# Squares of queries and keys one step later, GpSimd's weight additions ahead of modulation row loads

## The reference

```python
q = apply_rope(rmsnorm(heads(q, N_HEADS_A), qn), cos, sin) * scale
k = apply_rope(rmsnorm(heads(k, N_KV_A), kn), cos, sin)
...
s = jnp.einsum('bqhgd,bkhd->bhgqk', qi, k_all)
p = softmax_f32(s, v_all.dtype)
```

## Time and profile before

| | us |
|---|---|
| median of 3 runs | 2938.09 |
| lowest and highest | 2937.65 and 2938.37 |
| the profiled execution | 2939.53 |
| its span, first to last instruction | 2937.7 |
| TensorE busy | 2817.2 |
| VectorE busy | 1363.4 |
| ScalarE busy | 770.1 |
| GpSimd busy | 225.2 |

### The profile page before, as it was taken

The page is one execution under the profiler, slowest core; times in us unless marked ns, Lnnn a source line. Parts: engine busy times, 40 slices in busy tenths (PEclk is TensorE's granted clock), DMA queues, the critical chain, the costliest instruction groups (busy, mean ns, idle before and its releaser), DMA issues.

```text
span 2937.7 us, 33851 instructions
## 1 busy us (share of the span) xinstructions
PE 2817.2 (96%) x13312; PEld 1523.4 (52%) x13312; DVE 1363.4 (46%) x2569; ACT 770.1 (26%) x1410; POOL 225.2 (8%) x253
## 2 busy tenths in 40 slices
PE   7999899999999999999999989999999999999998
PEld 3555555655555655576444644444445734444442
DVE  2696776775355674674485741111115813121112
ACT  3334454441222453433251120000003232000001
POOL 2233212100011010000000000000002300000000
PEclk9999999999999999999999999999999999999999
DMA  8244222111145443112110158999993217999996
GB/s 315 90 162 153 91 73 87 37 73 58 79 155 169 135 152 106 44 46 89 63 61 20 56 216 359 421 421 422 421 420 145 107 67 299 410 421 422 421 421 282
DMA packets 90673, 586.60 MB, mean 200 GB/s; under 512 B 10192, under 2 KB 10192, under 8 KB 29232
## 3 DMA queue, kind: packets, MB, share of 16 engines
q1 hardware_dynamic: 69696, 502.56, 42.6%
q0 software_dynamic: 20848, 82.26, 8.4%
HBM read 582.68 MB, written 2.10 MB: 199 GB/s over the span
## 4 chain that ended last, share of the span: by engine, by line
PE 68%; DVE 6%; ACT 2%; issue 1%; DVEq 0%; ACTq 0%
PE BIG L1097 43%; PE PJ L1097 11%; PE BIG L1941 4%; PE PT L1426 2%; PE PT L1442 2%; DVE ARENA L2984 1%; PE PT L1097 1%; PE BIG L1409 1%; PE PJ L1146 1%; PE BIG L1413 1%; PE PT L1917 1%; DVE ARENA L3036 0%; DVE ARENA L3035 0%; ACT ARENA L2145 0%; PE BIG L1402 0%
## 5 line engine op out<-in xcount | busy, mean ns | idle before, releaser
L1097 PE MATMUL BIG<-ARENA 128*64 128x512 f32 (+3 forms) x2720 | 565.4, 458 | 6.5 <-DVE ARENA L3058 2.5
L1097 PEld LDWEIGHTS BIG<-ARENA 128*64 128x64 f32 (+1 forms) x2720 | 302.2, 169 | 255.4 <-issue 224.3
L1097 PE MATMUL PJ<-HT,W 128*128 128x512 f32 (+2 forms) x1040 | 400.3, 533 | 7.3 <-DVE ARENA L2694 2.6
L1097 PE MATMUL BIG<-W,ARENA 128*64 128x512 f32 (+1 forms) x1280 | 282.0, 573 | 0.9 <-DVE ARENA L2906 0.9
L1097 PEld LDWEIGHTS PJ<-HT,W 128*128 128x128 f32 x1040 | 193.8, 193 | 166.3 <-issue 127.9
L3087 DVE SCALAR_TENSOR_TENSOR XC<-BIG,MOD,XC 128x512 f32<-128x512 f32 x128 | 90.2, 747 | 379.4 <-PE BIG L1941 379.4
L2156 ACT ACTIVATE ARENA<-PT 128x512 f32<-128x512 f32 (+1 forms) x264 | 145.1, 583 | 416.8 <-PE PT L1426 416.5
L1097 PE MATMUL BIG<-HT,W 128*128 128x512 f32 (+1 forms) x600 | 236.6, 553 | 2.4 <-DVE ARENA L2860 2.1
L1097 PEld LDWEIGHTS BIG<-W,ARENA 128*64 128x64 f32 (+1 forms) x1280 | 107.4, 142 | 161.0 <-issue 154.9
L2723 DVE TENSOR_REDUCE STAT<-BIG 128x1 f32<-128x512 f32 (+5 forms) x240 | 169.9, 724 | 39.2 <-PE BIG L1413 34.2
L1097 PE MATMUL BIG<-HT,ARENA 128*64 128x512 f32 (+1 forms) x632 | 182.9, 573 | 0.0
(11 more groups left out here) (325 smaller groups left out, 3068.4 us busy)
## 6 DMA issues: line engine op xcount, KB each, us to landing
ARENA<-in_exp_w SPq DMA_DIRECT2D x168, 1024.0 KB, 18.1
W<-in_exp_w SPq DMA_DIRECT2D x144, 1024.0 KB, 16.7
W<-in_units SPq DMA_DIRECT2D x89, 1024.0 KB, 4.9
HT<-in_exp_w SPq DMA_DIRECT2D x72, 1024.0 KB, 21.9
ARENA<-in_mod_rows POOLq DMA_DIRECT2D x76, 512.0 KB, 4.5
W<-in_mod_rows POOLq DMA_DIRECT2D x52, 512.0 KB, 4.5
ARENA<-in_bias_b POOLq DMA_DIRECT2D x16, 384.0 KB, 4.9
XC<-in_x SPq DMA_DIRECT2D x1, 3072.0 KB, 10.1
```

The lines of the kernel that those rows point to most:

```text
L1097: ins = pe.matmul(out, lhsT, rhs, start=start, stop=stop, skip_group_check=skip)
```

## The change

In `block_slots` an item "square" no longer takes the place of its turn: it is put into the step behind that of the item before it, at most `room - 1`, and the norm that follows it comes no earlier than that step. Items behind the square keep their places. In GpSimd's list each unit's additions are sorted 16 places before the end of position 5 of the unit before, instead of at it; what they wait for stays the same.

```diff
@@ block_slots
     room = tiles if PAIRS[i][0] == "B" else tiles - 1
+    squared = 0
...
             least = before + 1
             continue
+        if item[0] == "square":
+            squared = min(before + 1, room - 1)
+            out.append((squared, item))
+            continue
+        if item[0].startswith("norm_"):
+            at = least = max(at, squared)
         out.append((at, item))
         before = at
@@ gpsimd program
+            ADDED_AHEAD = 16
             jobs = [(row_place(x)[0], 1, x) for x in range(len(MOD_ROWS))]
...
             for u in range(len(uses)):
-                jobs.append((uses[u - 1][5][1] if u else -1, 3, u))
+                jobs.append((uses[u - 1][5][1] - ADDED_AHEAD if u else -1, 3, u))
```

## The result

The changed kernel took 2947.86 us (median of five runs, 2947.69 to 2953.07) against 2938.09 us: a ratio of 1.0039, 95% interval 1.0028 to 1.005. It is slower by about 9.8 us; 13.7 were forecast, and the range of 2944.0 to 2958.0 holds the time. The profiled execution took 2947.69 us with a span of 2945.9, so it is 8.16 us longer than that of before. In the changed kernel the numbers of the lines are 8 higher than before (L1097 is L1105, L2091 is L2099, L2156 is L2164, L2177 is L2185, L1354 is L1362, L2613 is L2621); on GpSimd they are 7 higher (L1007 is L1014).

A forecast was written before the change was run, and what follows sets the result against it. TensorE, busy 96% of the span, was taken as the bound, so its waits decide. Terms 8.3 + 2.8 - 0.8 + 2.1 + 1.3 = +13.7 us gave 2951.8 us against the median of 2938.09, range 2944.0 to 2958.0.

The forecast's parts named there:

- the main term: Layer 0, second modulation vectors: their load goes behind unit 7's additions, ScalarE's Silu starts 8.3 us late, TensorE takes it all.
- the squares win: Rival, pairs 5 to 7: second norm matmul starts about 0.8 us sooner in each; 2947.6 us in all; chance 0.06.
- vectors that are late but cheap: Rival: vectors' load lands in 4.9 or 6.4 us, without the clock's 2.8; 2945.7 to 2947.2 us; chance 0.13.
- Vectors late: ScalarE's Silu on the second modulation vectors: load issued 13.2 us later, lands after 8.2, Silu 8.3 us late (6.5 to 10.8).
- rival of the cheap load: Rival at the second vectors' load: landing in 4.9 or 6.4 us, no slow clock; 2945.7 to 2947.2 us; chance 0.13.
- Clock behind the gap: TensorE after its 9.2 us idle gap: granted clock at 0.50 for 5.70 us, losing 2.8 us (0 to 3.4).
- Key square: Pair 4: square and table load stand before the copy of product 4, delaying the second norm matmul; loss 2.1 us.
- Units 2 and 4: Additions there skip a row load's wait, VectorE comes free about 0.4 us sooner at L2613 waits; gain 0.8 us in all.
- Pairs 5 to 7: Query squares cost 0.2 us in each, earlier additions 0.4 in pairs 5 and 7; loss 1.3 us (0.3 to 2.5).

The follow-up runs named there:

- e3: Changed kernel with the squares put back where they were, so only the additions sorted 16 places ahead: 2949.27 us, ratio 1.0039.
- e1: Changed kernel with additions sorted 15 places ahead instead of 16, squares as changed: 2942.85 us, ratio 1.0016.
- e5: Changed kernel with ScalarE's work on the second modulation vectors (wait, table load, Silu) one step later in its program: 2943.02 us, ratio 1.0011.
- e9: Against the kernel before, only the additions of units 2 and 4 sorted 16 places ahead, no square moved: 2939.24 us, ratio 1.0003.
- e2: Changed kernel with the additions at their old places, so the moved squares alone: 2943.38 us, ratio 1.0019.
- e6: Changed kernel with additions 15 places ahead and each square directly in front of its normalisation, behind the copy of product 4: 2942.4 us, ratio 1.0011.
- e7: Changed kernel with additions 15 places ahead and only query squares moved, the key square at its old place: 2940.84 us, ratio 1.0002.
- e8: Changed kernel with additions 15 places ahead and no square moved: 2941.55 us, ratio 1.0004.
- e4: The changed kernel itself measured once more, nothing altered: 2950.95 us, ratio 1.0045.

## Why the prediction was right

The mechanism of the main term held at each step: the load stands behind the additions, ScalarE stands still at the Silu, and TensorE takes the whole wait. The smaller terms came out near their sizes, some of them in another place than was named. The time alone would not have told this: 2947.86 lies nearer to the times of two rivals (2947.6 for "the squares win", 2945.7 to 2947.2 for vectors that are late but cheap) than to the 2951.8 of the forecast; the traces and the runs rule these out. The terms of the sum against what was measured:

**Vectors late, 8.3 forecast: 8.3 measured.** The wait at the Silu is 8.31 in the changed kernel and 8.46 in e3, all of it passed on to TensorE (9.19 and 9.34 against 0.89), gone in e1 by one place of order, and gone in e5 without any change to GpSimd. The load took 8.2 us again, beside a SyncE load that took 7.4 instead of 4.9 (DMA issues of the changed kernel from 255 to 268):

```profile
W<-in_mod_vectors POOLq DMA_DIRECT2D x1, 1024.0 KB, 8.2
W<-in_units SPq DMA_DIRECT2D x1, 1024.0 KB, 7.4
```

That it was 8.2 once more is in part luck. The reason given was the row load just ahead of it; but near 248, with that same row load ahead, it took 8.2 and 8.6 in before and e9 and only 6.1 to 6.6 in e1, e2, e6, e7 and e8, and 6.2 would have made the term 6.3. In the late place it took 8.2 or 8.3 in all four profiles (the changed kernel, e3, e4, e5), each time beside the SyncE load, which took 7.3 or 7.4; that the two slow each other is likely by this, but not shown. The rival of the cheap load is out, and so is the estimate from the DMA page of the Trainium skill, 4.4 us for 1 MB ("DMA: Bandwidth & Descriptors", "Anatomy of one DMA — SWDGE (gpsimd) path"): the trace shows 8.2. No run here has this load alone.

**Clock behind the gap, 2.8: 2.8.** 13.24 - 8.3 - 2.15 = 2.8 in the changed kernel, 2.7 in e3. In e3 it is as forecast, 5.3 us of work at half behind the gap. In the changed kernel the size is in part luck: only 3.0 us of work at half stand behind the gap, worth 1.5, and about as much came from 296.8 on, in the waits that the key square makes (the same waits bring no fall in e1 and e2). The row that 2.8 was taken from the earlier trace rows also has only 4.45 us of work in its 5.70, worth 2.2.

**Key square, 2.1: 2.14 and 2.15** (e1 and e2), zero in e7. The step named the second norm matmul and the copy; in the trace the first norm matmul already waits for the square, 1.53 us, and only 0.68 falls to the second.

**Units 2 and 4, -0.8: -0.8.** By the start of the one matmul that waited and of the one ahead of it, 0.41 is won at each place in all nine profiles that have these additions ahead, and 0.0 in e2, which has not. The place was named wrongly: the waits for L2613 stayed (2.45 us at 231 us, as before); what went are two waits of 0.36 us for VectorE's addition (L2560) one product earlier. The slow clock behind unit 2's gap at 117.9, for which the prediction allowed up to 1.5 more, did stay away in the changed kernel and gave 1.5; but another stretch at 0.50 came at 231.9 and took 1.7, of which 0.7 came back at 244.

**Pairs 5 to 7, 1.3: 0.82.** The squares were mis-sized, 0.2 each against 0.06: the waits for square and copy that came (1.09 and 0.68 less 0.47) are just what the waits for L2156 were (1.28). The additions cost 0.32 each in pairs 5 and 7 against 0.4. "The squares win" is out, for no pair gains the 0.8 that it needs, and e6 gains no time by another order. The next instruction follows directly behind each 1.28 us table load, so the 2.66 us of the Trainium skill's page "ScalarE: Activation LUTs" ("What ACT_TABLE_LOAD costs") are not seen here.

These terms sum to 8.3 + 2.8 + 2.1 - 0.8 + 0.8 = 13.2 against 13.7. The profiled execution is only 8.16 us longer than that of before. Of the 5.1 between, 3.4 are slow clock elsewhere, which the sum took as unchanged: the profile of before has more of it between 292 and 363 us and near 1166, 1.7 us each. Another 1.3 lie in the start, which stays open, and 0.6 in the units, by the changes of the clock just told; 0.2 go the other way in the rest. The medians differ by 9.8 because that of before is 1.4 below its profiled execution. In e4 the same kernel lost 3.4 us more to the clock in the filters, and was 12.6 above before.

The changed kernel's first five runs lie at 2947.7 to 2947.9 and at 2952.8 to 2953.1. The second kind was not profiled, but the mean granted clock of each run is known: 0.990 in the first kind, 0.988 in the second. By an estimate 0.002 of 2950 us is 5.9 us of full clock lost, as much as lies between them to within the rounding; where it fell is not shown. In e7 the clock goes with the time as well, from 0.992 in the four runs of 2933.4 to 2935.6 to 0.988 in that of 2946.0. For the same reason the medians of e1, e2 and e8, which lie some 3 us above what their edits cost by the trace, stay open to that extent: most of their runs have 0.990, most of before's 0.991.

No version here beats the kernel before by what can be measured; the parts worth keeping, units 2 and 4, are worth 0.8 us by the trace, and e9, which keeps them alone, lost as much to the clock.

## What to carry to other kernels

When an in-order queue is re-sorted by a constant, list every job that changes sides, not the ones meant: here one place, 343 against 344, put a 1 MB load behind four additions and cost 11 of the 13 us, while 15 instead of 16 cost nothing there. A late load costs what stands behind its consumer in that engine's queue; moving the consumer one step (e5) was as good as restoring the load. For edits of a few us, compare kernels by the starts of the same instructions in their traces, since the granted clock far from the edit moves the total by as much or more: the twelve runs of e7 lie up to 12.6 us apart.

## What was not expected of the hardware

The granted clock stood at 0.50 (1.2 GHz) in stretches in which TensorE was busy without a pause: 13.5 us at 1562.7 in e1, 6.8 and 3.4 at 1597.1 and 1617.6 in e4. The nearest wait ahead of each is a short one for VectorE: 1.00 us, over at 1560.7, in e1; 0.70, over at 1596.1, and 2.11, over at 1617.3, in e4. So the clock falls behind waits far shorter than the gap of 9.2 us. The same wait of 2.11 us stands in the profile after, and there the clock stayed full at 1617.6, in another execution of one program (TensorE of e4, then of the profile after):

```profile
1617.29 7.97 PE L1105 MATMUL BIG<-HT,W 128*128 128x512 f32 x14 [2.11 <-DVE ARENA L2868]
```

```profile
1615.76 10.57 PE L1105 MATMUL BIG<-HT,W 128*128 128x512 f32 x24 [2.11 <-DVE ARENA L2868]
```

And the same 1 MB load from GpSimd's queue, issued near 248 us behind the same row load, landed after 8.2 us in before and 8.6 in e9, but after 6.1 to 6.6 in e1, e2, e6, e7 and e8, though e2 moves nothing that stands ahead of it; why is open.
